# Order of two steps on ScalarE and VectorE in the expert loop of a two-block network

## The reference, cut to what matters

```python
def hier_moe(h, p):
    ...
    def expert(acc, ew):
        wg, wu, wd, cw = ew
        hid = jax.nn.silu(t @ wg) * (t @ wu)
        return acc + (cw[:, None] * (hid @ wd)).astype(acc.dtype), None

    out, _ = lax.scan(expert, jnp.zeros(t.shape, jnp.float32),
                      (p["w_gate"], p["w_up"], p["w_down"], comb))
```

## Time and profile before

| | us |
|---|---|
| median of 3 executions | 2789.84 |
| lowest, highest | 2779.86, 2791.86 |
| span of the profiled execution | 2783.9 |
| TensorE busy (matmuls) | 2328.6 |
| VectorE busy | 1625.2 |
| GpSimd busy | 1323.9 |
| ScalarE busy | 1104.4 |

### The profile page before, as it was taken

One profiled execution on the slowest core, in us unless ns is written; L12 is line 12 of the kernel. 1 busy time (PEld: TensorE's weight loads), 2 busy tenths in 40 slices (PEclk: granted clock), 3 DMA queues, 4 the chain that ended last, 5 costly groups with the idle time before them and its releaser, 6 DMA issues.

```text
span 2783.9 us, 41385 instructions
## 1 busy us (share of the span) xinstructions
PE 2328.6 (84%) x15250; PEld 1960.5 (70%) x15250; DVE 1625.2 (58%) x2522; ACT 1104.4 (40%) x1581; POOL 1323.9 (48%) x744
## 2 busy tenths in 40 slices
PE   5998777788498767785999997768999799999998
PEld 2864545677385466674868995325899699887998
DVE  3488464477558545674247555996555755523654
ACT  3222533466433435764434442001443344444443
POOL 2320132588442336882654552874565256441553
PEclk7995888899797888997989998668999899999999
DMA  5258602699326037883405441001455244342442
GB/s 228 91 202 322 217 15 91 228 341 344 144 96 252 1 112 268 321 296 133 171 24 199 186 172 71 0 0 52 165 192 189 91 181 182 135 152 91 152 181 91
DMA packets 93047, 443.73 MB, mean 159 GB/s; under 512 B 9088, under 2 KB 25600, under 8 KB 56704
## 3 DMA queue, kind: packets, MB, share of 16 engines
q1 hardware_dynamic: 79104, 390.10, 38.6%
q0 software_dynamic: 8496, 31.99, 3.0%
q10 hardware_dynamic: 5328, 20.04, 1.8%
HBM read 401.20 MB, written 40.89 MB: 159 GB/s over the span
## 4 chain that ended last, share of the span: by engine, by line
PE 40%; DVE 5%; POOL 3%; ACT 2%; DVEq 2%; POOLq 1%; issue 1%; DMA 0%; ACTq 0%
PE bank L657 11%; PE bank L658 11%; PE bank L659 11%; POOL ring_halves L371 2%; PE bank L699 2%; ACT high L1212 1%; PE bank L1123 1%; POOLq L593 1%; DVEq L2179 1%; PE bank L1061 1%; DVE HT L1633 1%; POOLq L598 1%; PE bank L1038 1%; DVE rstd L1618 1%; PE bank L1051 1%
## 5 line engine op out<-in xcount | busy, mean ns | idle before, releaser
L371 POOL TENSOR_TENSOR ring_halves<-ring,high 128x1024 fp32r<-128x1024 f32 (+1 forms) x230 | 814.2, 3541 | 953.9 <-ACT high L1212 953.9
L657 PE MATMUL bank<-ssdb_halves,high 128*128 128x256 f32 (+1 forms) x2080 | 619.6, 298 | 65.8 <-DVE HT_halves L1627 34.8
L658 PE MATMUL bank<-HT_halves,high 128*128 128x256 f32 (+1 forms) x2096 | 627.4, 299 | 0.0
L659 PE MATMUL bank<-ssdb_halves,ring_halves 128*128 128x256 f32 (+1 forms) x2080 | 615.5, 296 | 0.0
L1212 ACT CAST high<-ring 128x2048 fp32r<-128x2048 f32 x230 | 438.0, 1906 | 89.7 <-PE bank L659 89.7
L657 PEld LDWEIGHTS bank<-ssdb_halves,high 128*128 128x128 f32 x2080 | 400.8, 193 | 90.5 <-issue 61.2
L371 DVE TENSOR_TENSOR ring_halves<-ring,high 128x1024 fp32r<-128x1024 f32 x200 | 279.5, 1398 | 248.0 <-ACT high L1212 247.9
L658 PEld LDWEIGHTS bank<-HT_halves,high 128*128 128x128 f32 x2096 | 402.6, 192 | 8.9
L659 PEld LDWEIGHTS bank<-ssdb_halves,ring_halves 128*128 128x128 f32 x2080 | 398.4, 192 | 9.6
L378 DVE TENSOR_TENSOR dring_halves<-dring,dhigh 128x512 fp32r<-128x512 f32 x152 | 309.6, 2037 | 53.1 <-ACT dhigh L1218 53.0
L378 POOL TENSOR_TENSOR dring_halves<-dring,dhigh 128x512 fp32r<-128x512 f32 x152 | 264.5, 1740 | 80.7 <-ACT dhigh L1218 80.6
(11 more groups left out here) (415 smaller groups left out, 4603.3 us busy)
## 6 DMA issues: line engine op xcount, KB each, us to landing
ring<-in_ffn SPq DMA_DIRECT2D x88, 1024.0 KB, 5.4
ring<-in_moe SPq DMA_DIRECT2D x64, 1024.0 KB, 7.3
ring<-in_ada SPq DMA_DIRECT2D x48, 1024.0 KB, 6.9
dring<-in_ffn_down SPq DMA_DIRECT2D x88, 512.0 KB, 3.6
dring<-in_moe_down SPq DMA_DIRECT2D x64, 512.0 KB, 4.6
ring<-in_foxin SPq DMA_DIRECT2D x24, 1024.0 KB, 4.8
ring<-in_win SPq DMA_DIRECT2D x22, 1024.0 KB, 4.8
zs_b<-x_slots POOLq DMA_DIRECT2D x32, 512.0 KB, 8.8
```

What stands on the lines that cost most here:

```text
L371: eng.tensor_tensor(low, w, h, ALU.subtract).then_inc(sem(f"low_{engine}"), 1)
L657: mm(o, a[0], b[0], start=first, stop=last and bool(kw), **kw)
L658: mm(o, a[0], b[1], start=False, stop=last and bool(kw), **kw)
L659: return mm(o, a[1], b[0], start=False, stop=last, **kw)
```

## The change

In each slice, on ScalarE and on VectorE, the step on the turned hidden units of slice j now stands before the step on weight tile j+2. The steps are the same, with the same semaphores. TensorE, GpSimd and SyncE have the same instructions in the same order as before.

```diff
@@ ScalarE, experts, one(j, g)
                     act_fn(gact[:, j % 2, 0:P], ps[4 + j % 2][:, 0:P], ACT.Silu).then_inc(sem("gate_act"), 1)
+                    act.wait_ge(sem("hid_turned"), hid_turned0 + j + 1 + RING * g)
+                    nc.scalar.copy(r(hid[:, j % 2, 0, 0:P]), ps[4 + j % 2][:, TCOLS:TCOLS + P]).then_inc(sem("hid_high"), 1)
                     if j + 2 < slices:
                         make_high(c0 + j + 2, g)
-                    act.wait_ge(sem("hid_turned"), hid_turned0 + j + 1 + RING * g)
-                    nc.scalar.copy(r(hid[:, j % 2, 0, 0:P]), ps[4 + j % 2][:, TCOLS:TCOLS + P]).then_inc(sem("hid_high"), 1)
@@ VectorE, experts, one(j, g)
                     tt(hrows[:, j % 2, :], gact[:, j % 2, 0:P], ps[4 + j % 2][:, P:TCOLS], ALU.mult).then_inc(sem("hid_raw"), 1)
-                    if j + 2 < slices:
-                        make_low(dve, "dve", c0 + j + 2, g)
                     dve.wait_ge(sem("hid_high"), hid_high0 + j + 1 + RING * g)
                     tt(r(hid[:, j % 2, 1, 0:P]), ps[4 + j % 2][:, TCOLS:TCOLS + P], hid[:, j % 2, 0, 0:P], ALU.subtract)\
                         .then_inc(sem("hidden"), 1)
+                    if j + 2 < slices:
+                        make_low(dve, "dve", c0 + j + 2, g)
```

## The result

| | before | changed |
|---|---|---|
| median, us | 2787.06 | 2883.30 |
| lowest, highest | 2779.86, 2791.86 | 2880.64, 2896.14 |
| executions | 4 | 4 |
| span of the profiled execution | 2783.9 | 2884.0 |

The changed kernel takes 1.0348 times as long, with a 95% interval of 1.0316 to 1.0379: 96 us more by the medians, 100 us by the profiled executions. The prediction was 2894 us, in a range from 2866 to 2928.

A forecast was written before the change was run, and what follows sets the result against it. The pace was taken to hang on how early ScalarE casts the weight tile. The ring's 81.7 us plus 23 us of clock made 105 us, 2895 from the 2790 median, given as 2894 us, range 2866 to 2928.

The forecast's parts named there:

- The waits: On TensorE: the wait for hidden units goes; each slice instead waits 1.8 to 2.8 us for the weight tile's low part.
- The ring: Transpose, ScalarE's two casts, GpSimd's half, first gate and up half, next transpose: 7.55 us a slice, 81.7 us more in all.
- The table loads: ScalarE's 1.28 us loads before every fourth Silu in the second loop: hidden within the 7.55 us slice.
- The spare 0.2 us: Margin in the second loop: with a table load the path to the transpose takes 7.35 us, inside 7.55.
- The clock: On TensorE in both loops: 1.2 GHz for a quarter of the time, costing 23 us; this forecast case had chance 0.55.
- the clock holds: Rival: TensorE's waits are too short or too far apart to lower its clock, 2872 us; chance 0.20.
- VectorE: Its swap alone takes 35 us off both loops if nothing else moves; its tile half's new place costs nothing.
- The clock falls as in that stretch: Rival: TensorE's clock averages 0.70 in the loops, as from 1720 to 1920, 2927 us; chance 0.13.
- low in every first half: Rival: every first half of gate and up runs at 1.2 GHz, 92 us more, 2964 us; chance 0.04.
- faster: Rival: waits for the hidden units go and the later casts hurt nobody, 2755 us; chance 0.03.
- nothing moves: Rival: the swap leaves the time as it was, 2790 us; chance 0.02.
- Only the even slices hold: Rival: only even slices' tile casts start later, by 0.95 us, 29 us in all, 2819 us; chance 0.03.

The follow-up runs named there:

- filled: The changed kernel with 12 more idle transposes per slice behind the down products, inside TensorE's wait: 2857.99 us, 1.0276 of the kernel before.
- act_only: The kernel before with only ScalarE's two steps swapped, VectorE's left as they were: 2905.86 us, 1.0448 of the kernel before.
- turn_first: The changed kernel with TensorE's transpose of slice j put before the first half of gate and up of slice j+1: 2855.66 us.
- after_store_later: The changed kernel with ScalarE's store of a finished block put behind Silu of the next slice: 2891.83 us, 1.0394 of the kernel before.
- dve_only: The kernel before with only VectorE's two steps swapped, ScalarE's left as they were: 2904.42 us, 1.0432 of the kernel before.
- swap_even: The kernel before with the steps swapped on both engines in even slices only: 2862.15 us, 1.0290 of the kernel before.

## Why the prediction was right, point by point

**The waits.** TensorE's wait for the hidden units went, and a wait for the low part of the tile came, 27 times a loop and up to 2.9 us. The prediction had 1.8 and 2.8 us in turn, and where the clock is high that is what stands there (1.90 at 650.26, 2.87 at 657.77); behind a slice at the low clock the wait is shorter, down to 0.6 us.

**The ring.** The sum of five steps was 7.55 us; filled measured 7.475. Over 60 slices that is 4.4 us less than I had. By its steps, the transpose to the first product took 5.97 us in the profile after, not 6.01, and where nothing was late a slice closed in 7.44. So the ring's share is 448.6 - 371.3 = 77.3 us and not 81.7. act_only and turn_first show that it runs where I put it: through ScalarE's order, and through TensorE's order of transpose and first half.

**The table loads** were covered, with both loops at 224.3 us in filled, and after_store_later gained nothing by losing them. The spare 0.2 us was enough.

**The clock.** Forecast was a quarter of the time at 1.2 GHz, a clock of 0.87, and 23 us. It was 0.88, and 24.1 us by filled. That it came so close is in part luck. The quarter was picked between two bounds and no row gave it; the row that I leaned on, 0.70 in another stretch with waits of 2.8 us, would have given 55 us. I had 1.54 us more for a first half at the low level, and it was 1.19 (2.73 less 1.54); all first halves together were 21 us longer, and the other 3 us fell elsewhere in the slices. I also read rows 1 and 2 too loosely: they show waits up to 1.8 us in the second loop at a clock of 1.00, not only up to 1.3, which speaks more for "the clock holds" than I allowed.

The rule of the Trainium skill, page "TensorE: Matmul & The Clock Gate", section "HAM oscillation — how this bites in real kernels", that the clock falls again in every tile, is given there for tiles whose matmuls are shorter than the wait for the next. Here TensorE works for 4.7 to 5.7 us in a slice and waits for at most 2.9, so this isn't that case, and I should not have drawn "every first half" from it. Nor was that borne out: the clock fell in some slices and not in others with the same wait (579.51 and 657.77), and was back at 2.4 GHz in between.

**VectorE.** The prediction said that its half of the change costs nothing and is worth 35 us if nothing else moves. In the whole change it is indeed a gain (act_only is 23 us slower than the change). Alone, it is none: dve_only loses 122 us of span, through the order in which VectorE and GpSimd start on a tile and the lower clock that comes with it. The prediction passed over that, as its start in the full change is not disturbed. It also said that VectorE's half of the tile starts as before; in odd slices it started 1 us ahead of GpSimd before, and now starts with it.

**The rivals.** The time alone doesn't part the forecast from "the clock holds": 2883 us lies midway between 2894 and 2872. The clock of 0.88 does, and filled: with the clock held the kernel takes 2858 us. "The clock falls as in that stretch" (0.70) and "low in every first half" (14 of 60 took over 2.5 us) are out by the same rows, and "faster" and "nothing moves" by the time. "Only the even slices hold" was priced on the hold alone; measured, the even slices alone lose 84 us (76 of them in the loops), and the odd ones 28, so the odd slices are held too.

**Size.** The forecast was 81.7 + 23 = 105 us. The loops gave 77.3 + 24.1 = 101.4 us, the two profiled spans 100.1 us and the medians 96 us. So the ring term was 4.4 us too large and the clock term 1.1 too small, and the other 5 us lie between the loops of one execution and the medians, where these runs can't place them.

## What to carry to other kernels

Before you move a small step with a wait in front of a large one, ask what the engine that it waits for needs from the large step: here the transpose waited, through TensorE's own order, for the tile that stood behind it on ScalarE, and a lead of 3 us turned into a ring. A wait that shows on TensorE (17.5 us) is not what the change is worth; the chain that sets the pace went past it. Taking the store out of that chain took 40 us off the two loops (13 of them in the first, where no table loads went with it); the swap alone was at best worth 35. And price a new wait twice on TensorE, once for its length and once for the clock that it can lower.

## What the runs showed of the hardware

Twelve idle transposes per slice, 1.3 us of useless work (a wait of 2.87 us became 1.57), took 24 us off the two loops of the changed kernel: the clock went from 0.88 to 1.00. In swap_even the clock cost more (44 us) than the hold that lowered it (32 us), though the waits of 2.87 us came only once in two slices, about 15 us. And a start 0.33 us later on VectorE, against GpSimd on the same tile, made its record 3.15 us long and not 1.22; in dve_only this came back in nearly every even slice.
